# First norm by pairs of tiles with six shift blocks made on TensorE, x loaded first, and two re-orderings at ScalarE's turnovers

## The reference

```python
def modulate(h, shift, scale):
    return h * (1 + scale[:, None, :]) + shift[:, None, :]
...
    c_act = jax.nn.silu(c)
...
        mod = c_act @ mod_w[i] + mod_b[i]
        sh1, sc1, g1, shm, scm, gm, sh2, sc2, g2 = jnp.split(mod, N_MOD, axis=-1)
        h = modulate(rmsnorm(x, ffn_norm_w[i, 0]), sh1, sc1)
        x = x + FFN_HALF * g1[:, None, :] * swiglu(h, ffn_w_gu[i, 0], ffn_w_down[i, 0])
```

## Time and profile before

| | us |
|---|---|
| median of three runs | 2113.88 (2113.77 to 2113.98) |
| the profiled execution, its own time | 2114.27 |
| its span in the profile | 2112.5 |
| TensorE busy | 2063.0, 98% of the span |
| VectorE busy | 1165.1 |
| ScalarE busy | 833.2 |

### The profile page before, as it was taken

The page is one execution under the profiler, slowest core; times in us unless marked ns, Lnnn a source line. Parts: engine busy times, 40 slices in busy tenths (PEclk is TensorE's granted clock), DMA queues, the critical chain, the costliest instruction groups (busy, mean ns, idle before and its releaser), DMA issues.

```text
span 2112.5 us, 27703 instructions
## 1 busy us (share of the span) xinstructions
PE 2063.0 (98%) x10450; PEld 1714.5 (81%) x10450; DVE 1165.1 (55%) x1808; ACT 833.2 (39%) x1296; POOL 4.7 (0%) x29
## 2 busy tenths in 40 slices
PE   4999999999999999999999999999999999999998
PEld 2888888987777778888888888888888788888887
DVE  6555556677777754555566663333337964333333
ACT  4222222467666753422222342223126853222222
POOL 0000000000000000000000000000000000000000
PEclk8999999999999999999999999999999999999999
DMA  7655557435334423455567533332331223322322
GB/s 295 213 187 196 199 188 269 141 108 160 105 111 130 129 70 110 139 186 192 199 216 262 182 100 99 99 98 86 115 109 52 61 60 100 99 92 90 117 90 70
DMA packets 83218, 291.75 MB, mean 138 GB/s; under 512 B 8896, under 2 KB 11712, under 8 KB 83008
## 3 DMA queue, kind: packets, MB, share of 16 engines
q1 hardware_dynamic: 82848, 290.49, 41.8%
q10 hardware_dynamic: 288, 0.13, 0.0%
HBM read 288.36 MB, written 2.23 MB: 138 GB/s over the span
## 4 chain that ended last, share of the span: by engine, by line
PE 89%; DVE 4%; ACT 3%; issue 2%; DMA 1%; SPq 1%; ACTq 0%; DVEq 0%
PE bank L232 28%; PE bank L234 28%; PE bank L233 28%; DVE w_lo_sb L227 1%; DMA first_mod<-w_mod 1%; ACT w_hi_sb L222 1%; PE bank L1346 1%; PE bank L723 1%; PE bank L714 1%; DVE bc L875 1%; PE bank L1361 1%; SPq L1653 1%; PE bank L1381 1%; ACT h_hi L410 1%; DVE tmp L397 1%
## 5 line engine op out<-in xcount | busy, mean ns | idle before, releaser
L232 PE MATMUL bank<-h_hi,w_hi_sb 128*128 128x512 f32 (+1 forms) x1984 | 759.6, 383 | 22.8 <-DVE h_lo L390 18.4
L234 PE MATMUL bank<-h_hi,w_lo_sb 128*128 128x512 f32 (+1 forms) x1984 | 747.2, 377 | 0.0
L233 PE MATMUL bank<-h_lo,w_hi_sb 128*128 128x512 f32 (+1 forms) x1984 | 747.0, 376 | 0.0
L227 DVE TENSOR_TENSOR w_lo_sb<-raw,w_hi_sb 128x1024 fp32r<-128x1024 f32 x356 | 421.4, 1197 | 108.0 <-ACT w_hi_sb L222 102.5
L232 PEld LDWEIGHTS bank<-h_hi,w_hi_sb 128*128 128x128 f32 x1984 | 374.2, 189 | 101.4 <-issue 23.0
L234 PEld LDWEIGHTS bank<-h_hi,w_lo_sb 128*128 128x128 f32 x1984 | 374.0, 188 | 68.6
L233 PEld LDWEIGHTS bank<-h_lo,w_hi_sb 128*128 128x128 f32 x1984 | 374.3, 189 | 66.6 <-issue 1.7
L222 ACT ACTIVATE w_hi_sb<-raw 128x1024 fp32r<-128x1024 f32 x356 | 353.8, 1027 | 70.1 <-PE bank L234 70.0
L637 DVE TENSOR_TENSOR tmp<-tmp,bank 128x512 f32<-128x512 f32 x88 | 60.5, 687 | 418.1 <-ACT tmp L597 216.5
L232 PE MATMUL bank<-a_hi,w_hi_sb 128*128 128x512 f32 (+1 forms) x792 | 290.7, 367 | 0.0
L234 PE MATMUL bank<-a_hi,w_lo_sb 128*128 128x512 f32 (+1 forms) x792 | 290.0, 366 | 0.0
(11 more groups left out here) (207 smaller groups left out, 1613.8 us busy)
## 6 DMA issues: line engine op xcount, KB each, us to landing
raw<-w_stream SPq DMA_DIRECT2D x356, 512.0 KB, 4.1
mod_raw<-w_mod SPq DMA_DIRECT2D x144, 512.0 KB, 4.6
first_mod<-w_mod SPq DMA_DIRECT2D x16, 512.0 KB, 14.5
sums<-sums_rows SPq DMA_DIRECT2D x7, 1024.0 KB, 8.9
decays<-decay_rows SPq DMA_DIRECT2D x8, 768.0 KB, 4.2
x_trunk<-x_in SPq DMA_DIRECT2D x1, 2048.0 KB, 10.5
trunk_out<-x_trunk SPq DMA_DIRECT2D x2, 512.0 KB, 2.8
trunk_out<-x_trunk SPq DMA_DIRECT2D x4, 256.0 KB, 2.1
```

What stands on the lines that cost most here:

```text
L227: nc.vector.tensor_tensor(w_lo_sb[:, s, 0:width], raw[:, s, 0:width], w_hi_sb[:, s, 0:width], ALU.subtract).then_inc(w_lo, 1)
L232: nc.tensor.matmul(ps, s_hi, m_hi, start=start, stop=False)
L233: nc.tensor.matmul(ps, s_hi, m_lo, start=False, stop=False)
L234: return nc.tensor.matmul(ps, s_lo, m_hi, start=False, stop=stop)
```

## The change

Three things are done.

The loads. SP issues a 32-fold copy of c (`c_32`, 131 KB), then x in two halves, then c, scale blocks 0 and 1, the columns, shift blocks 0 and 1, slabs 0 and 1, and then three times a group of two shift blocks (now 1 MB in another layout, `w_first`) and two scale blocks, with slabs 2 and 3 after the first group.

The first norm. VectorE makes scale blocks 0 and 1 and shift blocks 0 and 1 and at once norms tiles 0 and 1; then for each further pair of tiles it makes two scale blocks, gathers them, and norms the pair. The other six shift blocks are products on TensorE: per pair (`shift_rows`) 8 float32 matmuls with 32 columns of `c_32` as weights and 256 columns moving, in four groups of 32 rows; ScalarE copies the four partial rows out (`copy_rows`), and two matmuls of one column (`shift_columns`) add and turn them. TensorE's first quad (`first_quad`) takes the slab pairs interleaved: pair 1 (slabs 2 and 3) two k tiles behind pair 0. Twenty small matmuls of ones (`keep_warm`) stand before the sums of squares and sixteen after `rstd` is made. FFN 0 becomes halved.

The turnovers. ScalarE's load of the Ln table goes from behind the fourth tile of half 0 to behind the eighth. The copy of slab 2 goes from behind the sixth tile to behind the third in late turnovers and behind the eighth in the others; that of slab 3 from behind the seventh to behind the eighth. In the first norm the Ln table is loaded ahead of the wait for the sums.

```diff
+            for v in (M_SC1A, M_SH1A):
+                sum_of(v, 0)
+                sum_of(v, 1)
+            collect(0)
+            dve.wait_ge(rs_step, 2)
+            for b in range(DT // 2):
+                if b:
+                    sum_of(M_SC1A, 2 * b)
+                    sum_of(M_SC1A, 2 * b + 1)
+                    collect(b)
+                scaled(2 * b)
+                scaled(2 * b + 1)
+                if b < 2:
+                    prep_lo(dve, 0, 2 * b)
+                rest(2 * b)
+                if b < 2:
+                    prep_lo(dve, 0, 2 * b + 1)
+                rest(2 * b + 1)
...
+                if j == 2 and late:
+                    prep_hi(act, n1 // 4, 2)
                 if j == 3 and st == PAIR:
                     pair_square_half(act, 1)
-                if j == 3:
-                    log_tables()
                 if j == 4:
                     square_half(act, st, 1)
-                if j in (5, 6):
-                    prep_hi(act, n1 // 4, j - 3)
+                if j == DT - 1:
+                    if not late:
+                        prep_hi(act, n1 // 4, 2)
+                    prep_hi(act, n1 // 4, 3)
+                    log_tables()
...
+                for k in range(DT):
+                    g = slice(32 * (k % 4), 32 * (k % 4) + 32)
+                    mm = nc.tensor.matmul(bank[4 + b % 2][g, 0:2 * P], c_32[:, k, :], w[:, k * 2 * P:(k + 1) * 2 * P],
+                                          start=k < 4, stop=k >= 4)
+                mm.then_inc(rows_made, 1)
...
+            pair_step(0, 0)
+            shift_rows(1)
+            pair_step(0, 1)
+            shift_columns(1)
+            for b in range(2, DT // 2 + 1):
+                for k in (2 * b - 2, 2 * b - 1):
+                    more = b < DT // 2 and k % 2 == 0
+                    pair_step(0, k)
+                    if more:
+                        shift_rows(b)
+                    pair_step(1, k - 2)
+                    if more:
+                        shift_columns(b)
+            pair_step(1, 6)
+            pair_step(1, 7)
...
-            for m in range(8 * MOD_FIRST):
-                sp.dma_start(first_mod[:, m, :], w_mod[m]).then_inc(first_loaded[m], 16)
...
+            keep_warm(pe, 20)
             for j in range(DT):
                 pe.wait_ge(first_sq_ready, j + 1)
                 mm = nc.tensor.matmul(bank[6][:, :], ones[:, :], first_sq[:, j, :], start=(j == 0), stop=(j == DT - 1))
             mm.then_inc(stat_done, 1)
-            ffn_tensor(pe, 0, S_FFN0, 0, 1, mods0)
+            pe.wait_ge(rs_step, 2)
+            keep_warm(pe, 16)
+            pe.wait_ge(quarter_row, 5)
+            ffn_tensor(pe, 0, S_FFN0, 0, 1, mods0, halved=True)
```

More of the change, by code:

```diff
@@ L91, with trunk @@
 FIRST_LINE = 1248
-def trunk(nc, w_stream, w_mod, w_dt, x_in, c_in, cols_in, ssm_cols_in, ssm_rows_in, att_rows_in, out):
+def trunk(nc, w_stream, w_mod, w_first, w_dt, x_in, c_in, c_32_in, cols_in, ssm_cols_in, ssm_rows_in, att_rows_in, out):
     ctx = ExitStack()
@@ L565, in down_mod, with keep_warm, first_quad, pair_step @@
             return None if mod0 is None else mod0 + MOD_GU
+        def keep_warm(pe, count):
+            for _ in range(count):
+                nc.tensor.matmul(bank[7][:, 0:P], ones[:, :], ones[:, :], start=True, stop=True)
+        def first_quad(pe):
+            def pair_step(u, k):
+                pe.wait_ge(h_lo_ready, k + 1)
+                w = slice(k * P, (k + 1) * P)
+                for l in range(2 * u, 2 * u + 2):
+                    if k == 0:
+                        pe.wait_ge(w_lo, l + 1)
+                    mm = product3(bank[l][:, :], w_hi_sb[:, l, w], w_lo_sb[:, l, w], h_hi[:, k, :], h_lo[:, k, :],
+                                  k == 0, k == 7)
+                    if k == 7:
+                        mm.then_inc(slab_used, 1)
+            def shift_rows(b):
+                pe.wait_ge(first_loaded[2 * b], 16)
+                if b == 1:
+                    pe.wait_ge(c_32_ready, 1)
+                if b == 3:
+                    pe.wait_ge(rows_copied, 1)
+                w = first_mod[:, 2 * b:2 * b + 2, :].rearrange("p j d -> p (j d)")
+                for k in range(DT):
[3 more added lines that the diff above has]
+                mm.then_inc(rows_made, 1)
+            def shift_columns(b):
+                pe.wait_ge(rows_copied, b)
+                for t in range(2):
+                    mm = nc.tensor.matmul(bank[6 + b % 2][:, t:t + 1], shift_row[:, b % 2, t * P:(t + 1) * P],
+                                          spare[:, 16:17], start=True, stop=True)
+                mm.then_inc(shift_turned, 1)
+            pair_step(0, 0)
[13 more added lines that the diff above has]
+            pair_step(1, 7)
         def ffn_tensor(pe, k, n0, hs, st, mod0=None, halved=False):
@@ L570, in turn @@
                 ready = lambda j: pe.wait_ge(h_lo_ready, h_before[hs] + j + 1)
+                if first and k == 0:
+                    first_quad(pe)
+                    pe.wait_ge(a_ready, ONE + 1)
+                    return
                 if first:
@@ L1750, in _ @@
                 nc.gpsimd.memset(spare[:, n:n + 1], 0.0).then_inc(starts_at_one, 1)
+            nc.gpsimd.memset(spare[:, 16:17], 0.0).then_inc(quarter_row, 1)
+            pool.wait_ge(quarter_row, 1)
+            for g in range(4):
+                nc.gpsimd.memset(spare[32 * g:32 * g + 1, 16:17], 1.0).then_inc(quarter_row, 1)
+                pool.wait_ge(quarter_row, g + 2)
             for m, fill in ((after, 0.0), (upto, 1.0), (ident, 0.0)):
@@ L1787, in _, with copy_rows, between @@
             prep_hi(act, 0, 0)
[L1788 to L1791, removed]
+            def copy_rows(b):
+                act.wait_ge(rows_made, b)
+                if b == 3:
+                    act.wait_ge(shift_turned, 1)
+                nc.scalar.activation(shift_row[:, b % 2, :], bank[4 + b % 2][:, 0:2 * P], ACT.Copy).then_inc(rows_copied, 1)
+            def between(j):
+                if j == 1:
+                    prep_hi(act, 0, 1)
+                if j in (1, 3, 5):
+                    copy_rows(j // 2 + 1)
+                if j == 1:
+                    prep_hi(act, 0, 2)
+                    prep_hi(act, 0, 3)
+            norm_scalar(act, 0, M_SH1A, h_hi, None, between)
+            ffn_scalar(act, 0, S_FFN0, 1, mods0, halved=True, between=lambda: wdt_scalar(act))
             turn_over_scalar(act, 1, 1, M_SHMA, h_hi, S_IN, late=True)
@@ L1809, in _ @@
             dve.wait_ge(c_ready, 1)
[L1810 to L1822, removed]
+            first_norm_vector(dve)
+            ffn_vector(dve, 0, S_FFN0, M_G1A, 1, mods0, 1, halved=True, between=lambda: wdt_vector(dve))
             columns_vector(dve, 3, M_SCMA, col("nw_mix0"))
```

98 lines of the change are left out of this document (85 added, 13 removed).

## The result

The changed kernel takes 2099.59 us (median of 6 runs, 2098.34 to 2099.91) against 2113.86 of the kernel before (2113.77 to 2113.98): a ratio of 0.993 with a 95% interval of [0.992, 0.9941], 14.3 us faster. The forecast was 2102.4 with a range of 2096.5 to 2108.5. The profiled execution took 2098.47, its span is 2096.7.

The account below looks back on a forecast made before the run. TensorE was taken as the bound, so only its idle, half-clock or reducible work could gain. Start 5.5 plus turnovers 6.0 made 11.5 us, from the median 2113.88 to 2102.4, range 2096.5 to 2108.5.

Parts of the forecast that it names:

- the first rival: At the start, the clock stays up: start ends at 56.1, time 2099; four-at-once shift groups give 2099.5 too; chance 0.2.
- What bounds the kernel: Whole span: TensorE is busy for all but about 50 us; what is won ahead of its gapless stretches is kept.
- The second turn: Start of TensorE's second turn in FFN 0: from 65.03 to 59.5, a gain of 5.5 us.
- Loads and ScalarE at the start: First norm: 1.56 MB less before the squares saves 3.7 us; x complete at 9.5, loads stop being the limit.
- Sums of squares: TensorE in the first norm: small matmuls raise the clock, 8 x 0.86 brings the sums to 15.0.
- First pair: Start, pair 0: first `h_lo` at 21.8; clock falls after idleness, first k step ends at 24.8, against 23.7 without.
- The shift groups: TensorE at the start: 1.8 us per group of 16 passes, bounds 0.86 and 3.44; turning the rows costs 0.45.
- Half clock after the second stretch: Start, third k tile: after 4.2 us of TensorE idleness, half clock for some 4 us.
- The turnovers: Five turnovers: moving ScalarE's table load and slab copies lets TensorE start sooner, 6.0 us in sum (nothing to 7).
- The serial groups: Rival at the start: shift groups run in series, 3 x 1.64 more, time 2107.3; chance 0.1.
- The turnovers change nothing: Rival at the turnovers: no gain, since the half-1 norm falls behind instead, time 2108.4; chance 0.07.
- The slower case: At the start, every shift-group pass drains before the next: three groups add 18.1, time 2120.5; chance 0.02.

Follow-up runs that it names:

- run 2: The changed kernel with the old ScalarE order at the turnovers, so the new start alone (also written `start_only`): 2105.55 us.
- run 9: The changed kernel with 28 small matmuls straight after the sums instead of 16 after `rstd`, filling only the first idle stretch: 2098.44 us.
- Runs 5: The changed kernel with a shift group's eight products reordered so that two neighbours share a group of 32 rows: 2098.51 us.
- run 6: The changed kernel with all eight products of a shift group accumulated in the same 32 rows: 2107.54 us, one execution.
- Runs 8: The changed kernel with both idle stretches filled, 28 small matmuls after the sums and 16 ahead of the third k tile: 2096.98 us.
- runs 3 and 4: The kernel before with only the Ln table load moved (2111.07 us), then with only the copies of slabs 2 and 3 moved (2109.55 us).
- run 1: The kernel before with only ScalarE's new order at the five turnovers: 2107.66 us.
- run 10: The changed kernel with the six shift blocks made on VectorE again, everything else kept: 2101.04 us.

## Why the prediction was right, point by point

**The number.** 2099.59 measured against 2102.4: 14.3 us won and not 11.5. The turnovers were right to 0.1 or 0.2 us; nearly all of the miss is the start, forecast at 5.5 and worth 8.4. The range held because it took in shift groups from 0.86 to 3.44. The time is in fact that of the variant that I had put into the first rival, four groups at once (2099.5), and not that of my own working.

**What bounds the kernel.** Right. TensorE had no wait in FFN 0 after the start, nor in FFN 1 behind its turnover, and the halved FFN 0 cost nothing: of the 9.79 at the second turn the marker at 386.42 kept 9.73.

**The second turn.** Read wrongly in the trace of before (65.03 for 64.48), so that the difference to the 59.5 of my working was 4.9 and not 5.5. It came at 54.69. That is before 55, which I had named as a sign of being wrong, and it is one: no forecast k step was missing, but the shift groups and the half clock took less than I had them at, as follows.

**Loads and ScalarE at the start.** Squares began at 6.65 (forecast 7.0), the first block sum at 12.28 (12.8), `rstd` was ready at 17.7 (17.7). VectorE's four block sums ended at 17.5, so neither waited long for the other.

**Sums of squares.** Right: 7.03 us (6.9) at full clock behind small matmuls.

**First pair.** `h_lo` at 21.3 (21.8). The clock did not fall in the profiled execution, and the first FFN matmul was at 21.36, sooner than the 22 to 24 of the forecast; in others it fell, as assumed (run 2's profile; run 9 by the times). The price I gave (1.1 us at the first k step) is near the 1.3 us between the levels.

**The shift groups.** The step that was wrong in its reason. I took 1.8 us, from the thought that the list's order lets only neighbours overlap. Runs 5 and 6 show that groups work independently: 1.0 us. Three groups at 0.8 less are 2.4 us. I had the second of them at half clock besides (2.7, measured 1.04, since the clock was up again at 33.11), which is another 0.9: 3.3 us in all. In the profiled execution the first k step ended at 23.39 and not at 24.8, 1.4 sooner, mostly as the clock had not fallen; with the 3.3 that is 4.7 of the 4.8 us by which the second turn came before 59.5. Over the runs of `start_only`, most of them on the upper level, the start is worth 8.4: 4.9 + 3.3 = 8.2. The Trainium skill's figure, TensorEngine Tiling (Array Packing), Theoretical Speedup, up to 4x for 32-wide weights, would have been the better choice here: to the end of the last pass the traces have 3.64 us with one group and 1.07 with four, 3.4 times as long. Its note that tiles operate independently (Key Properties) agrees with run 5. The 0.45 for turning the rows came from no row; it measured 0.36 (35.54 to 35.90).

**Half clock after the second stretch.** Right in place, and nearly in length: 29.70 to 33.11, 3.4 us for the forecast 4. Runs 8 and 9 price it at 1.5 us. The forecast spent it on a k step and a group; in the trace it slowed the k step alone (30.14 to 33.00).

**The turnovers.** Forecast 1.45, 0.95, 0.85, 1.45, 1.25, sum 6.0; measured 1.64, 1.10, 0.93, 1.02, 1.41, sum 6.1, and 6.25 in medians. Turnover 4 was 0.4 short: there TensorE still waited 0.47 for an `h_lo`. It had the same wait for `h_lo` before, 0.47 at 1596.65, so I was wrong to take it as like turnover 1, whose wait of 0.36 is gone. My working counted table and copies together; runs 3 and 4 show that the table alone is worth 2.8 and the copies alone 4.3. The later Ln of half 1 stayed covered.

**The rivals.** The serial groups were priced at 2107.3; the run that forces them took 2107.54. That this agrees is luck: I added 4.9 us to a sum that was 2.8 too high, and the three groups really took 8.5 us more (3.57, 4.37 and 3.57 us to the next instruction, for 1.0). "The turnovers change nothing" fell in run 1. The quick clock (2099) is about where the lower level lies, by another way: there the clock fell at the second stretch, and the groups were short. The slower case, each pass draining, fell with the 1.0 us of a group.

## What to carry to other kernels

Where a pipeline starts with work on one engine whose results are needed tile by tile, make just what the first tiles need, and read the cost of every round from the engine that the next round waits for. In a turnover, write down the list of each engine between two tiles: a 1 us copy that is needed only later costs nearly as much in that place as a table load (here two copies 4.3 us over five turnovers, the table 2.8). In the two waits of 2.8 and 3.8 us here, small matmuls that lie wholly inside the wait bought 1.3 us (where the clock had fallen) and 1.5 us, and took away the scatter of the runs.

## What the runs showed of the hardware that was not expected

- Float32 products of 32-wide weights in four groups of 32 output rows run at once, whatever the order in the list: 16 passes of 256 columns take 1.00 and 1.02 us to the next instruction in two orders, and 3.57 when all are in one group.
- The same idle stretch of 2.79 us lets the granted clock fall in some executions and not in others (the 32 passes behind it 3.84 or 5.46 us), which shows as two levels of the time 1.3 us apart. It fell in one of the six profiles that have this stretch (run 2). In the six profiles with an unfilled stretch of 3.76 us the clock fell every time, from 2.3 us before TensorE resumed (run 6) to 0.8 us after (run 2), and in run 10 it also fell behind a wait of 2.36 us.
- The clock column of the table reads 1.00 in the first microseconds, where the distances of the matmuls are those of half pace (0.213 for 128 columns in the change).
